# Differential attention stage: scores over 128 rows, sums of squares one per quarter, one batch of roots

## What is computed

```python
q = rms_norm_2(q.reshape(B, S, H, 2, d), qn_g)          # d = 64, mean square over each 64 features
k = rms_norm_2(k.reshape(B, S, H, 2, d), kn_g)
s = jnp.einsum("bhmqd,bhmkd->bhmqk", qblk, kt) * scale   # m = 0, 1: the two maps
s = s + bias[None, :, None]                              # then masked where key > query
p = jax.nn.softmax(s, axis=-1)
a = p[:, :, 0] - lam * p[:, :, 1]
o = einsum("bhqk,bhkd->bhqd", a, vt)
o = rms_norm_2(o, subln_g) * (1.0 - lambda_init)
o = o * jax.nn.silu(gate)
```

## Time and profile before

| | |
|---|---|
| runs | 1361.42, 1361.53, 1353.58 us |
| the profiled execution | 1353.24 us, its span 1351.5 us |
| mean granted TensorE clock | 0.975 of full |
| TensorE busy | 1247.8 us (92%) |
| weight loads | 1027.1 us (76%) |
| VectorE busy | 844.3 us (62%) |
| ScalarE busy | 591.3 us (44%) |
| GpSimd busy | 60.6 us (4%) |

### The profile page before, as it was taken

The page is one execution under the profiler, slowest core; times in us unless marked ns, Lnnn a source line. Parts: engine busy times, 40 slices in busy tenths (PEclk is TensorE's granted clock), DMA queues, the critical chain, the costliest instruction groups (busy, mean ns, idle before and its releaser), DMA issues. The chain is left out here.

```text
span 1351.5 us, 17221 instructions
## 1 busy us (share of the span) xinstructions
PE 1247.8 (92%) x6582; PEld 1027.1 (76%) x6582; DVE 844.3 (62%) x1388; ACT 591.3 (44%) x1074; POOL 60.6 (4%) x60
## 2 busy tenths in 40 slices
PE   5979999987895999999999999999998899999998
PEld 5969788875794987777777767788776688588888
DVE  4786666656736134778777886688566665573341
ACT  6644364334534345456555546323554222462220
POOL 2019100000000000000000000000000000000001
PEclk9989999989997999999999999999998999999989
DMA  9874221200043121121021213322221322132321
GB/s 344 294 264 142 78 70 56 63 32 16 17 157 125 63 93 48 63 78 63 32 78 63 79 47 125 94 94 94 78 63 40 132 89 99 36 105 83 106 77 48
DMA packets 33075, 125.93 MB, mean 93 GB/s; under 512 B 3840, under 2 KB 4096, under 8 KB 32480
## 3 DMA queue, kind: packets, MB, share of 16 engines
q1 hardware_dynamic: 29520, 107.49, 24.4%
q0 software_dynamic: 3184, 17.01, 3.4%
q10 hardware_dynamic: 288, 0.31, 0.1%
HBM read 118.51 MB, written 6.29 MB: 92 GB/s over the span
## 5 line engine op out<-in xcount | busy, mean ns | idle before, releaser
L406 PE MATMUL bank<-hl,wh 128*128 128x512 f32 x880 | 367.3, 417 | 10.2 <-ACT th L973 4.7
L408 PE MATMUL bank<-hh,wh 128*128 128x512 f32 x880 | 346.8, 394 | 0.0
L407 PE MATMUL bank<-hh,wl 128*128 128x512 f32 x880 | 345.7, 393 | 0.0
L1508 DVE TENSOR_TENSOR wl<-raw,wh 128x1024 fp32r<-128x1024 f32 x179 | 217.6, 1240 | 110.0 <-ACT wh L945 107.7
L945 ACT ACTIVATE wh<-raw 128x1024 fp32r<-128x1024 f32 x179 | 184.3, 1054 | 213.8 <-PE bank L408 195.6
L406 PEld LDWEIGHTS bank<-hl,wh 128*128 128x128 f32 x880 | 167.4, 190 | 51.5 <-issue 17.0
L407 PEld LDWEIGHTS bank<-hh,wl 128*128 128x128 f32 x880 | 167.6, 190 | 35.9 <-issue 6.0
L408 PEld LDWEIGHTS bank<-hh,wh 128*128 128x128 f32 x880 | 166.7, 189 | 37.0
L1859 DVE SCALAR_TENSOR_TENSOR ca<-u,vt,ca 128x512 f32<-128x512 f32 x232 | 158.0, 747 | 0.0
L406 PE MATMUL bank<-wl,hh 128*128 128x256 f32 (+1 forms) x352 | 103.3, 293 | 7.3 <-DVE cumt L1595 4.8
L407 PE MATMUL bank<-wh,hl 128*128 128x256 f32 (+1 forms) x352 | 101.4, 288 | 0.0
(11 more groups left out here) (288 smaller groups left out, 2034.0 us busy)
## 6 DMA issues: line engine op xcount, KB each, us to landing
raw<-in_chunks SPq DMA_DIRECT2D x203, 512.0 KB, 3.8
x<-in_x POOLq DMA_DIRECT2D x4, 512.0 KB, 10.4
mem_scratch<-kvm POOLq DMA_DIRECT2D x1, 2048.0 KB, 7.2
x<-in_x POOLq DMA_DIRECT2D x1, 2048.0 KB, 8.1
x_scratch<-x POOLq DMA_DIRECT2D x1, 2048.0 KB, 6.5
kvm<-mem_scratch POOLq DMA_DIRECT2D x1, 2048.0 KB, 8.3
x1r<-x_scratch POOLq DMA_DIRECT2D x1, 2048.0 KB, 8.6
out_x<-x1r POOLq DMA_DIRECT2D x8, 256.0 KB, 2.5
```

The lines of the kernel that those rows point to most:

```text
L406: pe.matmul(o, a[0], b[1], start=start, stop=False, **kw)
L407: pe.matmul(o, a[1], b[0], start=False, stop=False, **kw)
L408: return pe.matmul(o, a[0], b[0], start=False, stop=stop, **kw)
L1508: dve.tensor_tensor(wl[:, w], raw[:, NRAW[nxt] % RAWS], wh[:, w].bitcast(F32), ALU.subtract)\
```

## The change

- Scores use all 128 rows. Keys lie whole in a new array `kd` (two copies, for even and odd heads, in memory that block 1's `x` has left and `y` takes later). Queries go into `qz`, map 0 in one slot and map 1 in the other, whose other 64 rows are still block 1's zeros. So there are three copies and three subtractions a head in place of two and two (`split_head`; `split_keys`, `split_queries`), and the counts that others wait for change from 2 to 3 a head.
- The sum over squared queries moves from the fourth to the second quarter, behind its fourth piece, and that of squared keys to the third, behind its fourth piece. Each waits for its square.
- ScalarE reads each sum out of bank 7 with an Identity (scaled, plus epsilon) at the start of the second and third quarter (`mean_of`), ahead of that quarter's exponentials.
- In the third quarter, right behind the gate's tanh and ahead of the transposed probabilities, one logarithm and one exponential over all rows of `norms` that hold sums make the roots (`roots_together`). The one-column logarithm goes.
- The convolution's input was already first in VectorE's last quarter, and that stays.

```diff
-                    pe.wait_ge(s.q_lo, Q1 + 2 * j + 2)
+                    pe.wait_ge(s.q_lo, Q1 + 3 * j + 3)
                 for m in range(2):
                     b = 2 + 2 * (u_ % 2) + m
-                    half = slice(HD * m, HD * m + HD)
                     banks.open(pe, b, ("D", u_, m))
                     o = ps[b][:, 0:w]
-                    three(o, (qh[half, q_], ql[half, q_]), (kh[half, 0:w], kl[half, 0:w]), True, False)
+                    three(o, (qz[:, m, 0, q_], qz[:, m, 1, q_]), (kd[:, j % 2, 0, 0:w], kd[:, j % 2, 1, 0:w]), True, False)
...
-                    for i in range(2):
-                        pieces(fill, at + min(2, half // 2) * i, min(2, half // 2))
-                        if tt == 3 and j < 7:
-                            pe.wait_ge(s.squared, 4 + 2 + 2 * j + i + 1)
-                            total(("dns", 2 * j + 2 + i), [norms[:, i, :]], blocks)
+                    pieces(fill, at, min(4, half))
+                    if tt in (1, 2) and j < 7:
+                        pe.wait_ge(s.squared, 4 + 2 + 2 * j + tt)
+                        total(("dns", 2 * j + 1 + tt), [norms[:, tt - 1, :]], blocks)
...
+            def mean_of(key, dst, n):
+
+                banks.wait_full(act, key)
+                banks.empty(act.activation(dst, ps[7][:], ACT.Identity, scale=1.0 / n, bias=eps6), key)
+
+            def roots_together(keys, rows):
+
+                for key in keys:
+                    banks.wait_empty(act, key)
+                logs[0] += 1
+                act.activation(rows, rows, ACT.Ln).then_inc(s.logged, 1)
+                act.wait_ge(s.logged, logs[0])
+                act.activation(rows, rows, ACT.Exp, scale=-0.5).then_inc(s.rms_done, 1)
+                rms[0] += 1
...
+            def split_head(j, last_scores):
+
+                act.activation(kd[:, j % 2, 0, :], qf[:, 1, :], ACT.Copy).then_inc(s.q_hi, 1)
+                banks.wait_full(act, last_scores)
+                for m in range(2):
+                    half = slice(HD * m, HD * m + HD)
+                    act.activation(qz[half, m, 0, :], qf[half, 0, :], ACT.Copy).then_inc(s.q_hi, 1)
...
+                    if tt == 1 and j < 7:
+                        mean_of(("dns", 2 * j + 2), norms[:, 0, :], HD)
+                    if tt == 2 and j > 0:
+                        mean_of(("sub", j - 1), rs, P)
+                    if tt == 2 and j < 7:
+                        mean_of(("dns", 2 * j + 3), norms[:, 1, :], HD)
...
                     if tt == 2:
                         banks.empty(tanh_of(("gb", j)), ("gb", j))
                         th_free[0] = ("ga", j)
-                        act.activation(warm, eps6, ACT.Ln)
+                        roots_together(([("sub", j - 1)] if j else []) + ([("dns", 2 * j + 2 + i) for i in range(2)] if j < 7 else []),
+                                       norms[:, 0 if j < 7 else 2:3 if j else 2, :])
                     if u_ > 0:
                         diff_pt_hi(u_ - 1)
                     if tt == 2:
                         split_v(dv[:, :, j * P:j * P + P], ("DO", j - 1) if j else ("PO", 15))
-                        roots_of(*([(("sub", j - 1), rs, P)] if j else []),
-                                 *([(("dns", 2 * j + 2 + i), norms[:, i, :], HD) for i in range(2)] if j < 7 else []))
                         ahead(("gb", j))
...
+            def split_keys(j):
+
+                dve.wait_ge(s.q_hi, Q1 + 3 * j + 1)
+                dve.tensor_tensor(kd[:, j % 2, 1, :], qf[:, 1, :], kd[:, j % 2, 0, :].bitcast(F32), ALU.subtract)\
+                   .then_inc(s.q_lo, 1)
+
+            def split_queries(j):
+
+                for m in range(2):
+                    half = slice(HD * m, HD * m + HD)
+                    dve.wait_ge(s.q_hi, Q1 + 3 * j + 2 + m)
+                    dve.tensor_tensor(qz[half, m, 1, :], qf[half, 0, :], qz[half, m, 0, :].bitcast(F32), ALU.subtract)\
+                       .then_inc(s.q_lo, 1)
...
                     if tt == 3 and j < 7:
-                        for i in range(2):
-                            split_q(i, Q1 + 2 * (j + 1) + i + 1, qf[:, i, :])
+                        split_keys(j + 1)
+                        split_queries(j + 1)
```

More of the change, by code:

```diff
@@ L127 @@
     "h_tmp": "chunks scaled and shifted", "dve_step": "VectorE's own steps", "sumsq": "rows of squares summed",
-    "ms_done": "mean squares of block 1's tail", "sqrt_done": "their roots", "rms_done": "1 / rms taken on ScalarE",
+    "ms_done": "mean squares of block 1's tail", "sqrt_done": "their roots", "logged": "logarithms of mean squares", "rms_done": "1 / rms taken on ScalarE",
     "nk_done": "memory tiles normalised", "xn_done": "token tiles normalised (x, then x1)",
@@ L324, in build @@
             [("u", [P, C, PAD + S], F32)])
-        cos, sin, gzb, rot, sel, x, xT, y = shared([("cos", [P, S], F32), ("sin", [P, S], F32), ("gzb", [P, 4, S], F32),
+        cos, sin, gzb, rot, sel, x, xT, kd, y = shared([("cos", [P, S], F32), ("sin", [P, S], F32), ("gzb", [P, 4, S], F32),
                                                ("rot", [P, P], F32), ("sel", [P, 8, P], BF16)],
                                               [("x", [P, T, D], F32)],
-                                              [("xT", [P, C, S], F32)], [("y", [P, C, S], F32)])
+                                              [("xT", [P, C, S], F32)], [("kd", [P, 2, 2, S], F32R)],
+                                              [("y", [P, C, S], F32)])
         cst = sb("cst", [P, K_BLOCKS])
@@ L752, in x_scores @@
                 if pr == 0:
-                    pe.wait_ge(s.q_lo, Q1 + 16 + 2 * h + 2)
+                    pe.wait_ge(s.q_lo, Q1 + 24 + 2 * h + 2)
                     pe.wait_ge(s.memk_lo, h + 1)
@@ L956, in roots_of @@
                     rms[0] += 1
+                    roots[key] = rms[0]
+            logs = [0]
+            def mean_of(key, dst, n):
[9 more added lines that the diff above has]
+                rms[0] += 1
+                for key in keys:
                     roots[key] = rms[0]
@@ L1269, in _ @@
                     act.wait_ge(s.qn_done, 2)
-                    for i in range(2):
-                        split_q(i, qf[:, i, :], ("S", UNITS - 1))
+                    act.wait_ge(s.x1_out, 16)
+                    act.wait_ge(s.zeroed, 1)
+                    split_head(0, ("S", UNITS - 1))
             def of_copy(j):
@@ L1295, in _ @@
                             act.wait_ge(s.qn_done, 2 * j + 4)
-                            for i in range(2):
-                                split_q(i, qf[:, i, :], ("D", u_, 1))
+                            split_head(j + 1, ("D", u_, 1))
                     for m in range(2):
@@ L1314, in _ @@
                         key = (("dq", "dk")[tt], j + 1)
-                        raw_q(key, tt, Q1 + 2 * j + 2)
+                        raw_q(key, tt, Q1 + 3 * j + 3)
                         banks.wait_empty(act, key)
@@ L1369, in diff_tail @@
                 for i in range(2):
-                    raw_q(("xq", i), i, Q1 + 16)
+                    raw_q(("xq", i), i, Q1 + 24)
                 x_squares(0)
@@ L1391, in _ @@
                     if pr == 0 and h < 3:
-                        raw_q(("xq", 2 * h + 2), 0, Q1 + 16 + 2 * h + 2)
+                        raw_q(("xq", 2 * h + 2), 0, Q1 + 24 + 2 * h + 2)
                     if (h, pr) == (3, 0):
@@ L1408, in _ @@
                     if pr == 0 and h < 3:
-                        raw_q(("xq", 2 * h + 3), 1, Q1 + 16 + 2 * h + 2)
+                        raw_q(("xq", 2 * h + 3), 1, Q1 + 24 + 2 * h + 2)
                         x_squares(h + 1)
@@ L1837, in _ @@
                 if g == 3:
-                    for i in range(2):
-                        split_q(i, Q1 + 1 + i, qf[:, i, :])
+                    split_keys(0)
+                    split_queries(0)
             taps_done = [0]
@@ L1979, in x_split @@
                 for i in range(2):
-                    split_q(i, Q1 + 16 + 2 * h + i + 1, qf[:, i, :])
+                    split_q(i, Q1 + 24 + 2 * h + i + 1, qf[:, i, :])
                 dve.wait_ge(s.memk_hi, h + 1)
```

## The result

Median 1366.09 us of nine runs (1363.54 to 1372.49), beside 1358.02 of nine runs before (1353.58 to 1361.62). The ratio is 1.0077 with an interval of [1.0057, 1.0096]: 8 to 13 us slower. The forecast was 1362 and +5.8.

A forecast was written before the change was run, and what follows sets the result against it. TensorE was taken to set the head's time; after the change, a ring through VectorE and ScalarE. The running sum went +0.8, -1.3, +4.5 after five rings, +5.8 with head 7 and tail: 1362 us, between 1359.0 and 1367.2; range 1345 to 1375.

The forecast's parts named there:

- The ring: Loop per head through transposed probabilities, VectorE's tail, ScalarE's square and TensorE to the next X: 42.9 or 42.5 us, against 41.5.
- Head 0 to 1: Head without convolution or previous output: VectorE is ahead, so TensorE's own 41.0 less 2.1 us sets the next head.
- X: Start of VectorE's second row maximum of 384 columns, in a head's third quarter; the point from which times are counted.
- The tail: Behind head 7, roots of one row still precede the transposed probabilities and push VectorE back about 1.6 us; TensorE waits.
- TensorE sets the head's time: In heads 2 to 6 before the change, TensorE is busy 41.24 of 41.50 us and so sets their time.
- TensorE alone would need 38.9: TensorE's time per head without waits after the change: 41.5 - 2.08 - 0.48 = 38.9 us.
- The batch swaps one wait for another and gives nothing.: In the third quarter, VectorE waits 3.2 us for transposed probabilities where it waited 3.35 us for roots.
- The sum: All changes from entry to tail added up: total +5.8 us, giving 1362 us between two scales.
- (a): Rival: TensorE stays the bound and the gain arrives, about -16 us, 1337 or 1345; chance 0.12.
- (c): Rival: score rows are not the cause and save nothing; each ring 1.04 us longer, +12, 1365 to 1373; chance 0.07.
- (d): Rival: each table load costs 1.38 us more where not waited for; ring 45.4, 1373 to 1381; chance 0.04.
- (b): Rival: TensorE's pauses of 1.7 and 2.0 us lower its clock; +16, 1369 to 1377; chance 0.09.

The follow-up runs named there:

- e10_best: Changed kernel with batch behind the copies, taps in VectorE's wait, sums behind fifth pieces, gated-output subtraction later, and head 7's taps moved: 1340.54 us, ratio 0.9884.
- e4_scores_only: Kernel before with only 128-row scores and three splits; sums and roots unchanged: 1352.85 us, ratio 0.9970.
- e11_head7_taps: Changed kernel with head 7's four convolution taps moved from ahead of the first quarter's probabilities to behind the second quarter's: 1365.08 us, ratio 1.0058.
- e2_warm: Changed kernel with the batched roots behind the transposed probabilities' and values' copies, and the one-column logarithm back behind the tanh: 1343.96 us, ratio 0.9901.
- e5_half_rows: Changed kernel with scores back on 64 rows and two splits a head: 1367.46 us, ratio 1.0077.
- e8_gate_first: Changed kernel with VectorE's gated-output subtraction moved from ahead of the gate's read to behind the next head's first two row maxima: 1363.81 us, ratio 1.0050.
- e9_all_gate_first: Changed kernel with batch behind the copies, taps in VectorE's wait, sums behind fifth pieces, and gated-output subtraction behind the next row maxima: 1345.07 us, ratio 0.9927.
- e1_order: Changed kernel with the batched roots moved behind the transposed probabilities' and values' copies, one-column logarithm still left out: 1356.7 us, ratio 0.9998.
- e6_warm_fifth: Changed kernel with batch behind the copies, one-column logarithm back, and each sum over blocks behind its quarter's fifth piece, not fourth: 1343.78 us, ratio 0.9910.

## Why the prediction was right, and where it was not

**Right in size, and in the way round.** The ring: 42.65 and 43.03 measured, 42.5 and 42.9 forecast. Head 0 to 1: 38.98 for 38.9. Logarithm and exponential 1.49 each for 1.48. VectorE's wait 3.07 for 3.2; the copy of the transposed probabilities starts at X + 7.25 for 7.28. Full rows follow at 0.23 us. TensorE without waits 38.9 in the forecast, 39.15 a head in e10_best. The four parts of the ring are each within 0.14 us of the forecast (above), and the first sum does start right behind the square's end. The tail, from head 7's X to its last subtraction, grew by 1.65 (18.03 to 19.68) for 1.6.

**The step that failed: where TensorE waits.** The prediction followed the data alone (splits to scores, square to sum) and put TensorE's waits there, 1.7 and 2.0 us. None stands at the score products, and 0.12 at the first sum. The long ones stand earlier, at the first and the ninth piece, 2.12 and 1.21 as listed, for PSUM banks that VectorE reads late. Counted from start to start, TensorE loses 43.03 - 39.15 = 3.9 us a head where 3.7 was forecast. The way through the square does close last, so the sum came out by the ring that was forecast; but it does so by only 0.12 us, and that the second way, which the prediction left out, lay just below it is luck. The consequence is in "TensorE sets the head's time" and in "TensorE alone would need 38.9": the second is true, but the first left out that VectorE's ring through the gate's bank had 0.07 us of room before the change. e4_scores_only shows it: the gain of the 128 rows is waited away without any batch and without a sum in that part. The rows' 2.08 us in eight heads should have been some 16 us; alone they gave 4 (0.9970 of 1356.9, interval 0.9946 to 0.9994).

**"The batch swaps one wait for another and gives nothing."** Against before this is so: X to normalisation is 11.81 for 11.91. What it left out is that the same batch two instructions later, with its table loaded early, takes 8.83.

**The sum.** The forecast had +3.4 from head 0's X to head 7's: -2.1, five rings +5.8, head 7 -0.3. The profiled execution has 293.20 against 285.92, +7.28: -2.03, +6.73, +2.58. The rings are 0.9 too low in the forecast. 0.27 of this is the ring from head 2 to 3, 43.30 for 43.03: ahead of its normalisation VectorE has a plain tap where the other ring with a final add has the shorter first tap of a chunk (X + 12.08 for X + 11.81). It is not the clock, which fell in that ring: e11_head7_taps has 43.30 there too, at a clock of 1.00. Of head 7's miss of 2.9, 2.55 is the clock. As e11_head7_taps takes that pause away and gains only 1.0 in the median, most executions probably don't have this fall; that is not shown. At the entry, TensorE's wait for the splits grew from 1.88 to 2.59, the 0.6 of the forecast and 0.1; behind it to the first X it took 21.17 us where e2_warm, with the same instructions up to there and no fall of the clock, took 19.58. The first X itself lies 8 us later than before, but 5.3 of these lie ahead of any changed instruction, and among the kernels with the same code up to there that point lies up to 5.8 us apart. That is the scatter between executions, and the reason why 1362, between two scales, had to be that loose.

**The rivals.** (a) fell: the gain does not arrive. By the ring's sum the square alone would have stopped it, as forecast; in the trace the banks take most of it first. (c) fell: e4_scores_only and e5_half_rows turn 2.1 us on and off in head 0 to 1 with the rows. (d) fell: the tanh ends at 700.88 and the load starts at 700.90, the logarithm 0.01 behind its end. The Trainium skill (ScalarE: Activation LUTs, What ACT_TABLE_LOAD costs) puts draining beside the load; this case's traces show no gap for it. (b) was half right, at the wrong place and with too high a point. It expected a fall from pauses near 3 us on. A granted clock under 1.00 in this stage was also one of the prediction's own signs of being wrong, and it is there; TensorE idle ahead of the score products was one of its signs of being right, and it is not. The clock is not the change's loss either: e5_half_rows has the same ratio to before, and in its profile the clock stays at 1.00 throughout the stage.

## What to carry to other kernels

- An engine that is busy for 99% of a stretch need not be what sets its time: another engine's loop of the same length may lie under it. Walk one period round through every wait, buffers as well as data, and write down the room at each meeting point; with room of 0.07 us, 2.1 us a head taken off the busy engine gave nothing in these heads.
- When an instruction is put ahead of others on an in-order engine, list what stands behind it and who waits for that. Here the same batch stood at +8 us, at 0, or at -13 us against before: ahead of two copies, behind them, and behind them with its table loaded early.
- When two ways round are 0.1 us apart, removing one long wait only brings out the other, and an edit that moves both (e8_gate_first) can't say which one holds. Read the last wait before the period closes, even where it is shorter than a step.
- Work put into a wait on the other side (the four taps) does as well as removing the wait, and doing both adds nothing; check the last iteration by itself, where the pattern differs.

## What the runs showed of the hardware

TensorE's clock fell behind pauses shorter than expected, and not every time. In the changed kernel's profiled execution it fell three times in the stage, behind pauses of 2.59 (entry), 2.38 (a ring) and 2.62 us (head 7). The last, of head 7, in the stretch table, with the sum over blocks of two matmuls on TensorE's time line behind it, which takes 1.10 in other kernels:

```profile
812.00:815.00 3.00, 0.42 (x2) 0.38 (x3) 3.00 (x5) 0.11 (x1) 0.00 (x0) 1.00 0.31 98
815.00:823.00 8.00, 6.73 (x22) 4.83 (x21) 4.20 (x10) 2.85 (x8) 0.00 (x0) 0.57 0.25 94
```

```profile
818.56 2.05 PE L454 MATMUL bank<-norms,cst 128*128 128x512 f32 x2 [1.27 <-ACT mx L1304]
```

Over the profiles of all kernels here: at pauses of 2.59 to 2.64 us it fell in 12 of 18, at 2.12 to 2.39 in 5 of 9, and at none of 2.02 or less in this stage. It came down to 0.50, the 1.2 GHz level, and stayed there for about 3.5 us, but for 7 and 10 us in the two profiles where a second pause of 1.27 us came while it was down (after the change, and e9_all_gate_first). In e1_order, e2_warm and e6_warm_fifth that pause came just behind its return to 1.00, and it stayed up.

What a fall of 3.5 us costs depends on what waits behind it. At the stage's entry it is 1.6 us: 21.12 to 21.19 us to the first X in the kernels that have it, 19.56 and 19.58 in e11_head7_taps and e2_warm, which don't. In the ring from head 2 to 3 it cost nothing: TensorE's wait of 1.16 us for the gate's bank (e11_head7_taps, no fall) is gone in its place. In e8_gate_first, where that wait is 0.6, each fall cost 0.49.

A change of weights between 64 and 128 rows costs about 0.1 us (0.33 where 0.23 is the step); among full rows the step is 0.23, also here:

```profile
706.11 0.39 PE L407 MATMUL bank<-kd,qk 128*128 128x512 f32 x1
706.34 0.40 PE L408 MATMUL bank<-kd,qk 128*128 128x512 f32 x1
```
